# Moving the mask, the beta product and the query product of a chunked delta-rule stage from GpSimd to VectorE

## What is computed

```
g     = -exp(a_log) * softplus(a_lin + dt_bias);  beta = sigmoid(b_lin);  gc = cumsum(g) in a chunk
decay = exp(where(lower, gc[:, None] - gc[None, :], -inf))
a_mat = where(strict, (k * beta) @ k.T * decay, 0);   T = inv(a_mat + I)
u = T @ (v * beta);   w = T @ (k * beta * exp(gc));   qk = where(lower, q @ k.T * decay, 0)
for each chunk:   # state carried from chunk to chunk
    v_new = u - w @ state
    o     = (q * exp(gc)) @ state + qk @ v_new
    state = state * exp(g_last) + (k * exp(g_last - gc)).T @ v_new
```

## Time and profile before

| | |
|---|---|
| median of three runs | 2214.41 us |
| profiled execution | 2219.61 us, span 2217.8 us |
| TensorE busy (matmul) | 2064.5 us, 93% |
| VectorE busy | 1240.3 us, 56% |
| ScalarE busy | 847.0 us, 38% |
| GpSimd busy | 136.7 us, 6% |
| mean granted TensorE clock | 0.971 |

### The profile page before, as it was taken

One profiled execution on the slowest core, in us unless ns is written; L12 is line 12 of the kernel. 1 busy time (PEld: TensorE's weight loads), 2 busy tenths in 40 slices (PEclk: granted clock), 3 DMA queues, 4 the chain that ended last, 5 costly groups with the idle time before them and its releaser, 6 DMA issues. The chain is left out here.

```text
span 2217.8 us, 29438 instructions
## 1 busy us (share of the span) xinstructions
PE 2064.5 (93%) x11320; PEld 1631.7 (74%) x11320; DVE 1240.3 (56%) x2342; ACT 847.0 (38%) x1361; POOL 136.7 (6%) x114
## 2 busy tenths in 40 slices
PE   4979999998999999979999999999999898999998
PEld 2767878787878778856786787777776676788777
DVE  5867766685769576727625644445353333523453
ACT  3644342544354334127502333434444544500221
POOL 0020202020211111100000000000000000000000
PEclk7989999999999999999999999999999999999999
DMA  7322323232322232337313121120312115211232
GB/s 286 119 64 83 100 66 95 64 94 65 95 68 90 69 98 64 101 111 255 121 43 127 43 86 39 39 96 20 107 36 76 58 67 209 67 57 48 76 114 76
DMA packets 127674, 199.21 MB, mean 90 GB/s; under 512 B 56452, under 2 KB 87940, under 8 KB 126384
## 3 DMA queue, kind: packets, MB, share of 16 engines
q1 hardware_dynamic: 127536, 197.34, 27.3%
HBM read 155.17 MB, written 42.11 MB: 89 GB/s over the span
## 5 line engine op out<-in xcount | busy, mean ns | idle before, releaser
L779 PE MATMUL p_job<-h_hi,w_hi 128*128 128x512 f32 x768 | 324.9, 423 | 10.2 <-DVE kd L1040 6.8
L780 PE MATMUL p_job<-h_lo,w_hi 128*128 128x512 f32 x768 | 305.6, 398 | 0.0
L781 PE MATMUL p_job<-h_hi,w_lo 128*128 128x512 f32 x768 | 305.6, 398 | 0.0
L1630 PE MATMUL m_job<-h_hi,m_hi 128*128 128x512 f32 x576 | 251.0, 436 | 4.6 <-issue 3.9
L1632 PE MATMUL m_job<-h_hi,m_lo 128*128 128x512 f32 x576 | 229.1, 398 | 0.0
L1631 PE MATMUL m_job<-h_lo,m_hi 128*128 128x512 f32 x576 | 227.5, 395 | 0.0
L779 PEld LDWEIGHTS p_job<-h_hi,w_hi 128*128 128x128 f32 x768 | 148.1, 193 | 50.4 <-issue 15.7
L780 PEld LDWEIGHTS p_job<-h_lo,w_hi 128*128 128x128 f32 x768 | 148.6, 193 | 36.4 <-issue 7.9
L781 PEld LDWEIGHTS p_job<-h_hi,w_lo 128*128 128x128 f32 x768 | 148.0, 193 | 32.2
L1630 PEld LDWEIGHTS m_job<-h_hi,m_hi 128*128 128x128 f32 x576 | 110.0, 191 | 50.4 <-issue 31.2
L620 ACT ACTIVATE pre<-p_job 128x512 f32<-128x512 f32 x96 | 56.7, 592 | 199.1 <-PE p_job L781 197.7
(11 more groups left out here) (400 smaller groups left out, 4238.8 us busy)
## 6 DMA issues: line engine op xcount, KB each, us to landing
w_raw<-in_w SPq DMA_DIRECT2D x49, 512.0 KB, 3.7
m_raw<-in_w SPq DMA_DIRECT2D x49, 512.0 KB, 3.9
rows<-grows SPq DMA_DIRECT2D x32, 512.0 KB, 6.6
ada<-in_ada_w SPq DMA_DIRECT2D x8, 1024.0 KB, 7.7
z_scr<-pre SPq DMA_DIRECT2D x16, 512.0 KB, 2.6
o_scr<-oT SPq DMA_DIRECT2D x64, 128.0 KB, 1.8
ob<-o_scr SPq DMA_DIRECT2D x16, 512.0 KB, 3.8
zb<-z_scr SPq DMA_DIRECT2D x16, 512.0 KB, 4.7
```

The costliest lines, as they stand in the source:

```text
L779: nc.tensor.matmul(bank, hi, h_hi[:, k, cut], start=(k == 0), stop=False)
L780: nc.tensor.matmul(bank, hi, h_lo[:, k, cut], start=False, stop=False)
L781: last = nc.tensor.matmul(bank, lo, h_hi[:, k, cut], start=False, stop=(k == KD - 1))
L1630: nc.tensor.matmul(bank, hi, h_hi[:, k, cut], start=(k == 0), stop=False)
```

## The change

The three GpSimd steps go to VectorE, each at its place in the same list:

- `decay`: four `scalar_tensor_tensor` of 128 columns, which subtract the column (a scalar for each partition) and add the mask in one instruction. The GpSimd addition and the semaphore `diff_done` fall away.
- `dexp`: the two multiplications with beta, with the same waits, on VectorE.
- `queries`: the one multiplication of 2048 columns, with the same waits, on VectorE.

GpSimd keeps only the two memsets of this stage. `plan` is not changed, nor is anything on ScalarE, TensorE or SyncE.

```
@@ GpSimd program: removed
-                pool.wait_ge(cst, 48)
-                for i in range(N_IT):
-                    g = i - 1
-                    for s in plans[i]:
-                        if s[0] == "decay":
-                            b = s[2]
-                            pool.wait_ge(diff_done, 4 * i + b + 1)
-                            x = gams(i, b).rearrange("p a b c -> p (a b) c")
-                            nc.gpsimd.tensor_tensor(x, x, bc(tri[:], 1, 4), ALU.add).then_inc(mask_done, 1)
-                        elif s[0] == "dexp":
-                            ... (waits and two multiplications, as below on VectorE)
-                        elif s[0] == "queries":
-                            ... (as below)
@@ VectorE program, in step "decay", behind its waits
                             for a in range(2):
+                                for c in range(2):
+                                    t = 2 * b + c
+                                    last = nc.vector.scalar_tensor_tensor(
+                                        gam[:, slot(i, t), a, :], rows[:, 1, a, t * P:(t + 1) * P],
+                                        cols[:, t, 32 + 2 * i + a:33 + 2 * i + a], tri[:], ALU.subtract, ALU.add)
+                            last.then_inc(mask_done, 1)
+                        elif s[0] == "dexp":
+                            b = s[2]
+                            dve.wait_ge(decay_done, 4 * i + b + 1)
+                            if i >= 1:
+                                dve.wait_ge(merge_ready, 4 * g + 3)
+                            else:
+                                dve.wait_ge(rows_in, 64)
+                            for a in range(2):
                                 last = nc.vector.tensor_tensor(
-                                    gams(i, b)[:, :, a, :],
-                                    rows[:, 1, a, 2 * b * P:(2 * b + 2) * P].rearrange("p (c t) -> p c t", c=2),
-                                    bc(cols[:, 2 * b:2 * b + 2, 32 + 2 * i + a], 2, P), ALU.subtract)
-                            last.then_inc(diff_done, 1)
+                                    at[:, 2 * b:2 * b + 2, a, :], gams(i, b)[:, :, a, :],
+                                    rows[:, 0, a, 2 * b * P:(2 * b + 2) * P].rearrange("p (c t) -> p c t", c=2),
+                                    ALU.mult)
+                            last.then_inc(dbeta_done, 1)
+                        elif s[0] == "queries":
+                            dve.wait_ge(qexp, s[1] + 1)
+                            dve.wait_ge(nmul, 4 * (s[1] + 1))
+                            nc.vector.tensor_tensor(qd[:], qd[:], bc(qv[:, 0, :], 1, 2), ALU.mult).then_inc(qd_done, 1)
```

More of the change, by code:

```diff
@@ L430, in stage_deltanet @@
         rows_in = sem("b_rows")
-        diff_done = sem("b_diff"); mask_done = sem("b_mask"); decay_done = sem("b_decay"); dbeta_done = sem("b_dbeta")
+        mask_done = sem("b_mask"); decay_done = sem("b_decay"); dbeta_done = sem("b_dbeta")
         edge_dve = sem("b_edged"); edge_act = sem("b_edgea"); gl_done = sem("b_gl"); qexp = sem("b_qexp"); qd_done = sem("b_qd")
@@ L586, in _ @@
                 nc.gpsimd.memset(TD[:], 0.0).then_inc(u_zero, 1)
-                pool.wait_ge(cst, 48)
-                for i in range(N_IT):
-                    g = i - 1
-                    for s in plans[i]:
-                        if s[0] == "decay":
-                            b = s[2]
-                            pool.wait_ge(diff_done, 4 * i + b + 1)
-                            x = gams(i, b).rearrange("p a b c -> p (a b) c")
-                            nc.gpsimd.tensor_tensor(x, x, bc(tri[:], 1, 4), ALU.add).then_inc(mask_done, 1)
-                        elif s[0] == "dexp":
[L598 to L610, removed]
-                        elif s[0] == "queries":
-                            pool.wait_ge(qexp, s[1] + 1)
-                            pool.wait_ge(nmul, 4 * (s[1] + 1))
-                            nc.gpsimd.tensor_tensor(qd[:], qd[:], bc(qv[:, 0, :], 1, 2), ALU.mult).then_inc(qd_done, 1)
             @block.scalar
```

## The result

| | before | changed |
|---|---|---|
| median of the runs | 2216.91 us (4 runs) | 2253.53 us (4 runs) |
| ratio, 95% interval | | 1.0169 (1.0156 to 1.0182) |
| profiled span | 2217.8 us | 2251.8 us |
| the eight rings of chunk steps, together | 233.9 us | 272.5 us |
| the seven stretches of slices between them | 523.1 us | 522.6 us |

What follows compares the result with a forecast made beforehand. The prediction took the ring of engines waiting for each other, not the amount of work, to set the chunk steps' length. Its terms summed to +45 us on 2214.4, forecasting 2259.5 us, range 2237.5 to 2284 us, chance 0.62.

Steps and rivals of the forecast that it cites:

- decay in the ring: Before Dl of even chunks, four fused instructions replace two: +0.40 us each, 21 of them, +8.4 us (6.7 to 14.9).
- dexp b = 1 to 3: Between Dl and S of even chunks, VectorE waits for ScalarE's exponential: second S +0.53 us, 21 times, +11.1 us.
- dexp b = 0: Before a recurrence's first Dl, the product waits for table load and exponential: vn +1.9 us, seven times, +13.3 us.
- clock behind it: TensorE stands still some 3.4 us in the first step, its clock then falls: 1.7 us each, seven times, +12 us.
- queries of pair 0: The 2.3 us product stands ahead of grammul, so TensorE waits 4.7 us more: +4.7 us (4 to 5.5).
- iteration 0: Four decays and dexps among slices cost 4.3 us, but exponentials no longer wait for GpSimd's addition: 0 (-1 to +4).
- shorter waits for merge 1: In iterations 2, 4 and 6, TensorE's waits for VectorE get 1.5 us shorter each: -4.5 us (0 to -10).
- The ring: In chunk steps TensorE, VectorE and ScalarE wait for each other; whatever holds up Dl or S on VectorE lengthens the step.
- rule of half the rate: Rival: two fp32 SBUF sources halve the new decay's rate, 0.13 us more per instruction, 11 us: 2270.5 us, chance 0.06.
- What comes back: Without GpSimd's product beside it the cast takes 0.7 us, so VectorE's list is 1.9 us ahead at the lanes: -4.5 us.
- iteration 8's ring: Chunk steps that prepare nothing take 28.2 us against 29.0 in iteration 2, so the ring, not work, sets their length.
- The sum: All terms together: 8.4 + 11.1 + 13.3 + 12 + 4.7 + 0 - 4.5 = 45 us slower.

Runs made afterwards that it cites:

- e2: Kernel before with only the decay moved to VectorE as four fused instructions; mask addition gone, beta and query products stay on GpSimd: 2221.4 us, ratio 1.0026.
- e6: Changed kernel with only the beta product of b = 0 moved behind the write of chunk 0: 2230.3 us, ratio 1.0061.
- e5: Changed kernel with all four beta products moved behind the write of the same chunk, ScalarE's exponential left in place: 2226.3 us, ratio 1.0045.
- e4: Changed kernel plus 14 unread TensorE products between read and solve of the first chunk of rings 1 to 7: 2247.95 us, ratio 1.0147.
- e1: Kernel before with only the beta product (dexp) on VectorE; mask and query product stay on GpSimd: 2250.3 us, ratio 1.0158.
- e9: Kernel before with the exponential of b = 0 and GpSimd's product moved from ahead of the first read to between solve and write: 2204.8 us, ratio 0.9955.
- e7: Changed kernel with the queries step of pair 0 moved behind the four grammuls of pair 0: 2248.1 us, ratio 1.0148.
- e11: Kernel before, query product on VectorE, pair 0's behind its grammuls, b = 0 exponential moved, 12 unread products before merge 1 of iterations 2, 4, 6: 2199.3 us.

## Why the prediction was right, and where it was off

The direction, the mechanism in the rings and the order of the terms held; of what was to come back, next to nothing did. Term by term:

| term | forecast | measured | by |
|---|---|---|---|
| decay in the ring, 21 | +8.4 | +7.9 | e2's rings less those of before |
| dexp b = 1 to 3, 21 | +11.1 | +8.3 | e6's rings less e5's |
| dexp b = 0, 7 | +13.3 | +13.0 | e4's rings less e6's |
| clock behind it | +12 | +9.3 | changed rings less e4's |
| queries of pair 0 | +4.7 | +4.66 at the wait | 11.72 less 7.06 |
| iteration 0 | 0 | -2.1 | first decay to first gram product |
| shorter waits for merge 1 | -4.5 | -0.5; the waits themselves +1.8 | slices; 12.0 less 10.2 |

- *The ring.* The four measured parts make 38.5 us, the changed rings are 38.6 us longer. That is less of a proof than it looks: three of the four are differences along one chain of kernels and would add up whatever they were; what it tests is that e2's rings and e5's are the same. e1's rings are the independent check, with 34.7 us for `dexp` and its clock alone. The pitch of the fused instruction was right (0.26 against 0.25 us). The rule of half the rate for this form with two fp32 SBUF sources (the Trainium skill, Vector Engine (DVE) Microarchitecture Reference, section Points that are easy to get wrong) is not borne out: 128 columns take 346 ns, as `S` does with one input from PSUM, and L916 with 1024 columns 1.28 us.
- *dexp b = 1 to 3 (step mis-sized).* I put the delay of the second `S`, 0.53 us, at each. It is 0.40. The exponential starts 0.33 us behind `vn` instead of 0.42, and the products come 352.63 + 0.66 - 351.25 = 2.04 us behind `Dl`, where I had 2.17.
- *The clock (step mis-sized).* Seven falls of 1.7 us; the changed kernel has five (two rings are 33.85 us, as those with fillers) and they cost 1.3 to 2.4 us each.
- *Iteration 0.* I took 0. The first gram product comes at 126.78 instead of 130.32 us; 1.5 of the 3.5 us it already had at the first decay, from the stage in front. From the first decay to the first gram product it is 20.8 us instead of 22.8, and so it is in the other kernels: 22.6 to 22.9 us in the five with all of GpSimd's mask and beta work, 20.5 to 20.8 in the six with none. With these GpSimd instructions go slow-downs beside them: the kT norm product ran 1.25 us beside GpSimd and takes 0.68 now. I had this gain in the lower bound only as 1 us.
- *What comes back (the step that failed).* VectorE's list was to be 1.9 us ahead at the lanes, and TensorE's waits for merge 1 shorter by 1.5 us each. The list is ahead, up to the cast; then there is a new wait:

```profile
262.79 2.28 DVE L986 TENSOR_TENSOR qd<-qd,qv 128x2048 f32<-128x2048 f32 x1
264.98 0.69 DVE L897 CAST w_hi<-w_raw 128x1024 fp32r<-128x1024 f32 x1
265.70 1.23 DVE L899 TENSOR_TENSOR w_lo<-w_raw,w_hi 128x1024 fp32r<-128x1024 f32 x1
267.89 0.18 DVE L1044 TENSOR_TENSOR lane_tmp<-UL,AL 64x31 f32<-64x31 f32 x1 [0.97 <-DMA AL<-a_lanes]
```

The cast takes 0.69 instead of 4.88 us, but the lanes' load lands only now, and 0.97 us of the 1.9 go to it. Nor is what is left decided here. Shortly before merge 1 VectorE stands idle for the next weights, in the kernel before (first row) as in the changed one:

```profile
307.76 0.69 DVE L925 CAST w_hi<-w_raw 128x1024 fp32r<-128x1024 f32 x1 [3.15 <-DMA w_raw<-in_w]
314.32 0.69 DVE L897 CAST w_hi<-w_raw 128x1024 fp32r<-128x1024 f32 x1 [3.40 <-DMA w_raw<-in_w]
```

From this cast to the copy that merge 1 waits for, VectorE works without a gap (subtraction, three taps, decay, copy), and the same holds in iterations 4 and 6. So in the traces it is the landing of this load that sets VectorE's time at merge 1; I had not asked what is late next. How much of a lead the load passes on hangs on what starts it, which is not followed here. Counted from the end of the ring, the cast comes 0.7 us earlier (54.1 against 54.8), the decay in front of the copy takes 0.37 more, and the copy comes 0.3 us earlier (321.19 - 260.26 = 60.9 against 314.25 - 253.00 = 61.3). TensorE itself came 0.9 to 1.0 us earlier, and so its three waits grew, from 3.3, 3.1 and 3.9 us to 3.9, 3.6 and 4.5.
- *A reading that was wrong without harm.* I gave iteration 8's ring as 28.2 us; that stretch ran 3 us past its end. The bare ring takes 25.9 us, eight steps of 3.19 us and little more. The argument (a ring with nothing beside it is nearly as long) is weaker for it: the preparation costs 3.8 us of 29.7, of which e9 takes 1.0 away.
- *The sum.* 45 us forecast, 34.0 between the two profiled spans. Put in too high: dexp b = 1 to 3 by 2.8, the clock by 2.7, the other two terms of the ring by 0.8, everything up to the first ring by 3.8 (4.7 forecast, 0.9 measured, in which 1.5 us are the earlier start of the stage). Too low by 4.0: the slices, where 4.5 were to come back and 0.5 did. The remaining 4.9 us are the untouched code behind the stage, which ran shorter in that execution. Between the medians it is 36.6 us. Errors of both signs cancel here in part, so the total is nearer than the terms.

## What to carry to other kernels

Before an operation moves to another engine, look at what it waits for, and at who stands behind it in the new list: the beta product cost 35 us at one place (13 of them through the clock) and nothing in the rings one step later in the same list. A half-idle engine is not free where it is a link of a ring; an idle helper engine that only waits is worth more there than its speed says. And when an operation gets shorter, ask what its engine waits for next: half of the lead that the released cast gave went to one load, and a second load, for which VectorE had stood idle before as well, set the time at merge 1.

## What the runs showed of the hardware

- VectorE's fp32 cast beside GpSimd's product took 4.88 us and ended 0.55 us behind the product; without GpSimd beside it 0.69 us (mean of the 44 casts from 100 to 1010 us: 1.08 us before, 0.68 in the changed kernel). A product with two SBUF inputs was slowed beside GpSimd too (1.25 against 0.68 us for 512 columns), and where the VectorE instruction had started first, GpSimd's was: VectorE's 1024 columns from 116.09 us took their 1.28 us, GpSimd's addition from 116.25 us took 2.26 instead of 1.30; `S` and `Dl`, with one input from PSUM, were not (0.35 us beside GpSimd's L605 and without it).
- How often a wait of TensorE was followed by a lower granted clock (under 1.00 over the next 4 us), counted from the first ring to the last in all thirteen traces: 1.2 to 1.7 us, none of 14; 2.3 us, 23 of 39, with the same work around them; 3.3 to 3.4 us in the first step of a ring, 16 of 21 (five of the changed kernel's seven, e1 seven, e7 four); 3.0 us and more in front of merge 1, 36 of 36. Filled with unused products, the waits of the first step had none of seven (e4).
- What a fall avoided gives back in the total is less sure than in its place: 9.3 us in the rings were 5.6 us between the medians (e4), 5.7 us in three stretches were 1.7 us (e11), the latter inside the interval.
- A fused `scalar_tensor_tensor` of 128 fp32 columns with two SBUF inputs takes 0.35 us, 0.26 us from start to start.
